# One layer of a streaming encoder on one core: products grouped by operand part, the weights' low part last, and two low parts in one GpSimd operation

## The reference

```
h = rms_norm(x);  z = h @ w_in            # 2048 -> 512 + 512 + 64 + 5 x 2048 columns
q = rms_norm(z_q) @ w_q_b                 # 16 heads, 128 + 64 wide, rotary on the 64
k, v = rms_norm(z_kv) @ w_kv_b            # 16 heads, 128 + 128 wide
o = softmax(q k / sqrt(192), chunk-causal mask) v;   y_mla = (o * silu(g_mla)) @ w_o_mla
xc = conv4(u);  r, i = sigmoid(xc @ w_rg), sigmoid(xc @ w_ig)     # 16 blocks of 128
h_t = a_t h_(t-1) + sqrt(1 - a_t^2) i_t xc_t;        y_lru = (h * silu(g_lru)) @ w_o_lru
x = x + (sigmoid(m_mla) * y_mla + sigmoid(m_lru) * y_lru) @ w_out
x = x + (p @ w_ple) * sigmoid(rms_norm(x) @ w_ple_gate);   out = rms_norm(x)
```

## Time and profile before

| | |
|---|---|
| median of 3 runs | 1964.78 us (1964.34 to 1965.1) |
| profiled execution | 1965.18 us, of which 1963.5 us are the span from the first to the last instruction |
| TensorE's granted clock, mean over the span | 0.997 of full speed |
| busy | PE 1943.5 us (99%), DVE 1056.8 us (54%), ACT 792.6 us (40%), POOL 631.3 us (32%) |
| GpSimd's low parts in `low_parts` | 416, 564.6 us, 1362 ns each |
| GpSimd's idle time ahead of them | 1259.5 us, nearly all of it until ScalarE's copy |

### The profile page before, as it was taken

How to read it: one execution, slowest core, us unless ns; L and a number is a source line. 1 busy time by engine, 2 the same in 40 slices (tenths; PEclk the granted TensorE clock), 3 DMA queues, 4 the chain that set the end, 5 groups by cost and what they waited for, 6 DMA issues and landing times.

```text
span 1963.5 us, 27786 instructions
## 1 busy us (share of the span) xinstructions
PE 1943.5 (99%) x10762; PEld 1701.1 (87%) x10762; DVE 1056.8 (54%) x1559; ACT 792.6 (40%) x1276; POOL 631.3 (32%) x486
## 2 busy tenths in 40 slices
PE   9999999999999999999999999999999999999997
PEld 7889999999998888888888888888888888888885
DVE  5867778887883474477856657751111330112344
ACT  6434444443443455545345555422222222333323
POOL 3000000000003455355662222444444454444543
PEclk9999999999999999999999999999999999999998
DMA  7344444444445334334362423443333343225232
GB/s 291 110 128 128 140 119 140 129 129 136 121 132 168 122 108 150 108 129 132 88 166 71 143 94 140 146 166 129 107 128 129 128 172 107 86 88 213 86 107 107
DMA packets 211031, 256.25 MB, mean 131 GB/s; under 512 B 20797, under 2 KB 144357, under 8 KB 203621
## 3 DMA queue, kind: packets, MB, share of 16 engines
q1 hardware_dynamic: 195936, 185.11, 30.7%
q10 hardware_dynamic: 14981, 69.56, 9.5%
HBM read 218.45 MB, written 33.55 MB: 128 GB/s over the span
## 4 chain that ended last, share of the span: by engine, by line
issue 59%; PE 19%; POOL 18%; DVE 2%; ACT 1%; POOLq 1%; DMA 0%; DVEq 0%; ACTq 0%
PE ps L1662 19%; POOL wlo L429 18%; POOLq L428 0%; DVE xc L1334 0%; DVE ii L1333 0%; DMA praw<-in_p 0%; DVE gg L1337 0%; DVE tmp L1366 0%; ACT whi L519 0%; POOLq L494 0%; DVE x L1601 0%; DVE stage L1600 0%; ACT rr L689 0%; DVE latq L1344 0%; ACT hhi L549 0%
## 5 line engine op out<-in xcount | busy, mean ns | idle before, releaser
L429 POOL TENSOR_TENSOR wlo<-raw,whi 128x512 fp32r<-128x512 f32 x416 | 564.6, 1362 | 1259.5 <-ACT whi L519 1258.9
L519 ACT ACTIVATE whi<-raw 128x512 fp32r<-128x512 f32 x480 | 299.6, 631 | 777.8 <-PE ps L1662 728.0
L1662 PE MATMUL ps<-hhi,whi 128*128 128x512 f32 x640 | 249.7, 390 | 0.2 <-POOL wlo L429 0.2
L1662 PE MATMUL ps<-hhi,wlo 128*128 128x512 f32 x640 | 249.0, 389 | 0.0
L1662 PE MATMUL ps<-hlo,whi 128*128 128x512 f32 x640 | 249.0, 389 | 0.0
L1786 PE MATMUL ps<-shi,cut 128*128 128x256 f32 x768 | 217.3, 283 | 0.0
L1787 PE MATMUL ps<-slo,cut 128*128 128x256 f32 x768 | 217.3, 283 | 0.0
L1788 PE MATMUL ps<-shi,cut 128*128 128x256 f32 x768 | 217.3, 283 | 0.0
L643 ACT ACTIVATE cut<-wblock 128x768 fp32r<-128x768 f32 x96 | 81.1, 845 | 270.8 <-PE ps L1788 270.4
L1787 PE MATMUL ps<-hlo,cut 128*128 128x256 f32 x576 | 163.0, 283 | 0.0
L1788 PE MATMUL ps<-hhi,cut 128*128 128x256 f32 x576 | 163.0, 283 | 0.0
(11 more groups left out here) (293 smaller groups left out, 4151.8 us busy)
## 6 DMA issues: line engine op xcount, KB each, us to landing
wblock<-in_w_in SPq DMA_DIRECT2D x384, 128.0 KB, 2.5
raw<-in_w_in SPq DMA_DIRECT2D x40, 1024.0 KB, 5.0
raw<-in_w_o_lru SPq DMA_DIRECT2D x16, 1024.0 KB, 4.9
raw<-in_w_o_mla SPq DMA_DIRECT2D x16, 1024.0 KB, 4.9
raw<-in_w_out SPq DMA_DIRECT2D x16, 1024.0 KB, 4.9
raw<-in_w_ple_gate SPq DMA_DIRECT2D x16, 1024.0 KB, 5.0
gate_scr<-stage ACTq DMA_DIRECT2D x16, 512.0 KB, 3.6
raw<-in_w_kv_b SPq DMA_DIRECT2D x32, 256.0 KB, 4.0
```

The lines of the kernel that those rows point to most:

```text
L429: pool.tensor_tensor(wlo[:, k % RING], raw[:, k // RAWC, k % RAWC], whi[:, k % RING].bitcast(F32), ALU.subtract).then_inc(lo_ready, 1)
L519: act.activation(whi[:, c % RING], raw[:, c // RAWC % 2, c % RAWC], ACT.Copy).then_inc(hi_ready, 1)
L1662: return pe.matmul(o, l, r, start=start, stop=stop)
```

## The change

Three things change. `low_parts` works on two neighbouring chunks at once: it waits until both are copied, subtracts 1024 columns in one operation and counts `lo_ready` up by two. `features` and `tokens` go over the four pieces once for each product: high·high, then the product with the activations' low part, then the one with the weights' low part. And `chunk` waits for `hi_ready` at its first matmul and for `lo_ready` only ahead of the third product. `pt_lo` is waited for chunk by chunk in the first group. `new_values`, `keys`, `next_chunk` and the last tiles' loop stay as they are, as do `ple_low`, L459 and L488.

```diff
             def low_parts(c0, i):
-                for k in range(2 * RAWC):
-                    pool.wait_ge(hi_ready, i * (2 * RAWC) + (c0 + k + 1))
-                    pool.tensor_tensor(wlo[:, k % RING], raw[:, k // RAWC, k % RAWC],
-                                       whi[:, k % RING].bitcast(F32), ALU.subtract).then_inc(lo_ready, 1)
+                for k in range(0, 2 * RAWC, 2):
+                    pool.wait_ge(hi_ready, i * (2 * RAWC) + (c0 + k + 2))
+                    two, of_row = slice(k % RING, k % RING + 2), slice(k % RAWC, k % RAWC + 2)
+                    pool.tensor_tensor(wlo[:, two], raw[:, k // RAWC, of_row],
+                                       whi[:, two].bitcast(F32), ALU.subtract).then_inc(lo_ready, 2)
...
-            def tokens(s, slot, ahi, alo, first, last):
-                for m in range(4):
-                    o = ps[:, 4 * s + m]
-                    h, l = ahi[:, m * P:(m + 1) * P], alo[:, m * P:(m + 1) * P]
-                    mm(o, h, whi[:, slot], first, False)
-                    mm(o, h, wlo[:, slot], False, False)
-                    ins = mm(o, l, whi[:, slot], False, last)
+            def tokens(s, slot, k, ahi, alo, lo_made, last):
+                cols = [(ps[:, 4 * s + m], ahi[:, m * P:(m + 1) * P], alo[:, m * P:(m + 1) * P]) for m in range(4)]
+                for o, h, l in cols:
+                    mm(o, h, whi[:, slot], k == 0, False)
+                for o, h, l in cols:
+                    mm(o, l, whi[:, slot], False, False)
+                pe.wait_ge(lo_ready, lo_made)
+                for o, h, l in cols:
+                    ins = mm(o, h, wlo[:, slot], False, last)
                 return ins
...
             def chunk(c, what, s, ahi, alo, k, kn, i=0, stride=0):
-                pe.wait_ge(lo_ready, i * stride + (c + 1))
-                what(s, c % RING, ahi, alo, k == 0, k == kn - 1).then_inc(chunk_used, 1)
+                pe.wait_ge(hi_ready, i * stride + (c + 1))
+                what(s, c % RING, k, ahi, alo, i * stride + (c + 1), k == kn - 1).then_inc(chunk_used, 1)
...
-            pe.wait_ge(pt_lo, KP)
             def ple(g, s, k):
+                if g == 0:
+                    pe.wait_ge(pt_lo, k + 1)
                 chunk(C_PLE + g * KP + k, tokens, s, pthi[:, k], ptlo[:, k], k, KP)
```

More of the change, by code:

```diff
@@ L1662, in mm, with features @@
                 return pe.matmul(o, l, r, start=start, stop=stop)
-            def features(s, slot, ahi, alo, first, last):
-                for m in range(4):
-                    o = ps[:, 4 * s + m]
-                    h, l = whi[:, slot, m * P:(m + 1) * P], wlo[:, slot, m * P:(m + 1) * P]
-                    mm(o, h, ahi, first, False)
+            def features(s, slot, k, ahi, alo, lo_made, last):
+                rows = [(ps[:, 4 * s + m], whi[:, slot, m * P:(m + 1) * P], wlo[:, slot, m * P:(m + 1) * P]) for m in range(4)]
+                for o, h, l in rows:
+                    mm(o, h, ahi, k == 0, False)
+                for o, h, l in rows:
                     mm(o, h, alo, False, False)
+                pe.wait_ge(lo_ready, lo_made)
+                for o, h, l in rows:
                     ins = mm(o, l, ahi, False, last)
                 return ins
-            def tokens(s, slot, ahi, alo, first, last):
-                for m in range(4):
-                    o = ps[:, 4 * s + m]
-                    h, l = ahi[:, m * P:(m + 1) * P], alo[:, m * P:(m + 1) * P]
-                    mm(o, h, whi[:, slot], first, False)
-                    mm(o, h, wlo[:, slot], False, False)
-                    ins = mm(o, l, whi[:, slot], False, last)
+            def tokens(s, slot, k, ahi, alo, lo_made, last):
[4 more added lines that the diff above has]
+                    mm(o, l, whi[:, slot], False, False)
+                pe.wait_ge(lo_ready, lo_made)
+                for o, h, l in cols:
+                    ins = mm(o, h, wlo[:, slot], False, last)
                 return ins
```

## The result

| | median us | runs | over before |
|---|---|---|---|
| before | 1964.87 | 1964.34 to 1965.10 (4) | |
| changed | 1974.96 | 1974.38 to 1975.73 (4) | +10.1 |

The ratio is 1.0051, with a 95% interval of 1.0039 to 1.0063: slower, by more than what can be told from no change. The forecast was 1972.0, with 1967.5 to 1978. The profiled execution took 1975.08 us, its span 1973.3, which is 9.8 more than before.

What follows compares the result with a forecast made beforehand. TensorE, busy 99% of the span with a fixed sum of matmuls, was taken as the bound. Terms summed to +7.2 us on the profiled 1965.18, giving 1972.4; less 0.4 for the runs' median, 1972.0, range 1967.5 to 1978.

Steps and rivals of the forecast that it cites:

- The pair's cost: GpSimd's subtraction of 1024 columns: taken as 2.48 us, with ends 2.03 and 2.58.
- Values, end, chunk 40: TensorE's low-part waits: attention values, four times, +3.5 us; kernel's end, +1.9; recurrence's start at chunk 40, -0.2.
- `lru_decay` and `merge_gate_back`: Late pairs behind each `lru_decay`, four times, +0.8 us together; behind `merge_gate_back`, once, +0.4.
- the handover of 0.2: From a subtraction's end to TensorE's matmuls: 0.2 us added to each late pair.
- Stream: TensorE's steady matmuls: number and sizes unchanged, distance still 0.226 us, late pairs hidden with more than 3 us left.
- The order's gain: Rival, matmuls sharing the streamed operand: shorter gaps make the kernel faster, 1952 us at 4 ns each; 4%.
- the second wait's cost: Second wait in each chunk: taken as zero; as a rival, 20 ns in some 400 chunks, +8, 1980 us; 4%.
- `krw2`: VectorE's product and the chain ahead of it, held by longer GpSimd operations: +0.8 us, between a 1.0 gain and +3.6.
- three holds that are 1.2 longer: Upper end at `krw2`: VectorE's chain of scans and sums meets three longer GpSimd holds, +3.6 us.
- The third rival: VectorE's recurrence chains several us late, `gates` and `krw2` stand, ScalarE's copies behind `merge_gate_back` too: about 1977 us; 14%.
- Start: TensorE's first chunk can begin about 1.4 us sooner, but it then idles waiting for scaled x: 0.
- none of them behind TensorE: At the start: the transfers and ScalarE's squares ahead of VectorE's scaling of x don't wait on TensorE; gain 0.

Runs made afterwards that it cites:

- e3: Changed kernel with single low parts in the attention groups' chunks 176 to 223 and the last eight, 472 to 479: 1970.26 us, +5.3 over before.
- e2: Changed kernel with the old `low_parts`, so the new order of products alone: 1963.75 us, -1.2 against before.
- e10: Changed kernel, all pairs kept, with the square's sum and `krw2`'s products behind the second latent group's chunk 13 instead of 11: 1969.69 us, +5.2 over before.
- e7: Changed kernel with TensorE's first product held until the patch tokens' and first weights' low parts are there, as before the change: 1975.65 us, +10.9 over before.
- e11: The changed kernel as it is, timed again in a later set: 1974.68 us, +10.2 over before.
- e5: Changed kernel with single low parts in chunks 148 to 151 alone, beside `krw`: 1971.68 us, +7.0 over before.
- e12: Changed kernel with 24 transposes of the identity in TensorE's stand at `krw2`, timed beside the changed kernel: 1974.40 us, +9.9 over before.
- e1: Kernel before with the new `low_parts` (pairs) alone, products in the old order: 1983.09 us, +18.2 over before.

## Why the prediction was right, and where not

The sign, the size within 3 us and the mechanism held: TensorE's stream is a fixed sum, the pairs add waits in about ten places, and nothing in the new order makes up for it. The size was helped by luck: one term was 4.0 too small, and a gain that was put at nothing took 1.0 of that back.

- **The pair's cost.** Taken 2.48, measured 2.40 undisturbed (bounds 2.03 to 2.58). The estimate from the figure of the Trainium skill (GPSIMD Engine Reference, "Elementwise — side-by-side cycle accounting") was 2.36. The runs lie between.
- **Values, end, chunk 40.** +3.6, +1.8 and -0.2 against 3.5, 1.9 and -0.2; e3, with both removed, gains 4.8 over the changed kernel. The fourth group was 0.3 worse than the three others.
- **`lru_decay` and `merge_gate_back`.** +0.5 and +0.1 against 0.8 and 0.4: the shorter pair, and where it was just in time the handover of 0.2 didn't show in full. (The prediction has the pair end at 694.88; by its own 2.48 it is 694.86, less than 0.1 over the four.) These waits are too short for TensorE's list, which has 4.3 us in five waits on low parts where the forecast was some 7 in ten places.
- **Stream.** 0 as said. The order's gain and the second wait's cost are both nothing (e2).
- **`krw2`: the term that was mis-sized**, +4.8 against +0.8. The prediction had the mechanism, and as its bound "three holds that are 1.2 longer", +3.6. It took 0.8 as the middle of a range, where the trace had the operations in a row: no row of VectorE from 909 to 931 has idle time ahead of it, so that what is added ahead is passed on. What was added there is 1.3, not 3.6, since two of the three longer holds replaced shorter ones that had stood beside the next operation. `krw` itself met a pair from its start, 1.3 more, and TensorE came 0.5 sooner, which the sum had at nothing here. The stands came to 3.2; that this lies just under the bound is luck, its parts are others. The other 1.6 had no term: the granted clock. The third rival, "the long hold decides", named this place and about 5 us; its price was right only with the clock, which it didn't name, and its other two places (`gates`, the copies) stayed quiet.
- **Start: the other one**, -1.0 against 0. The step that failed is "none of them behind TensorE". VectorE's work on x is behind its copy of `vec`, in VectorE's own row of instructions, and `vec` is behind TensorE's first chunk. I had followed what x needs, and not what stands ahead of it in the queue.

Together: +4.0 at `krw2`, -1.0 at the start, -0.6 in the small places, which is the 2.4 by which the sum, 7.2, fell short of 9.6.

The Trainium skill (SBUF — State Buffer, "SBUF: two separate sides") has VectorE's two-input operation and GpSimd's exclude each other for a whole instruction. The rows bear it out for `krw` (3.41 us beside a pair that started 0.02 us sooner and ended at 930.16; its own length is about 1.2, by the 1.22 mean of the same form for `cut`). The cast, with one input, is held as well: 0.43 alone and 1.71 beside a pair. The same sentence of the page counts VectorE's operations in a two-port mode too; which mode the cast ran in, the rows don't tell.

## What to carry to other kernels

Before merging two operations on an engine that is not the bound, ask for each result when its reader asks for it: merging saves nothing there and delays the first half until the second's input is there and the longer operation is done. Price a longer shared hold by the chain behind it: where the held engine has no idle time up to the next hand-over, each longer hold is passed on, less the holds that fall away because the meetings are fewer; how much sooner the reader comes is added, and a stand of several us may cost the clock on top. If a late producer can't be helped, move the consumer in the other engine's row (e10: five of ten us back by one number).

## What the runs showed of the hardware

- TensorE's granted clock fell to its lower level behind stands (times over the stream's distance): after 1.4 and 2.7 us with two matmuls between (the four profiles that have these: the changed kernel, e3, e7, e11), after 1.4 and 1.3 (e5, in its profile), and after one of 2.0 (e12, at the end) or 1.9 us (e1). After other single stands of 1.8 to 2.0 us it did not (the changed kernel's end, e1's four `lru_decay` places), so the length of a single stand doesn't decide it in these traces. Each time it lasted some 3 us and cost about 1.5. e1 at the recurrence's start:

```profile
612.00:615.50 3.50, 3.50 (x10) 2.74 (x11) 2.48 (x4) 0.80 (x1) 2.15 (x1) 0.59 0.16 19
```

- VectorE's operations that met a pair are 1.1 to 1.3 us longer than beside a single subtraction or alone, and the pair is 1.1 longer. But there are half as many meetings, and VectorE's busy time over the whole kernel fell by 3 us. What counts is where they fall.
